# Layer 1's probabilities times v as three products of halves, and PSUM banks of layer 0 emptied ahead of the weight halves

## The reference, cut to what matters

```python
for layer in range(DEPTH):
    mod = cond @ ada_w[layer] + ada_b[layer]
    shift, scale, gate = jnp.split(mod, 3, axis=-1)
    h = rms_norm(x, norm_w[layer]) * (1.0 + scale[:, None, :]) + shift[:, None, :]
    y = moba_branch(...) if layer % N_MIXERS == 0 else mlstm_branch(...)
    x = x + gate[:, None, :] * y
# mlstm, one head: a causal decay matrix times q k^T, and that times v
s_qk = jnp.einsum('bhtd,bhsd->bhts', qc, kc) * jnp.exp(log_D - m_t[..., None])
num = (w_inter[..., None] * jnp.einsum('bhtd,bhde->bhte', qc, C)
       + jnp.einsum('bhts,bhse->bhte', s_qk, vc))
```

## Time and profile before

| | us |
|---|---|
| median of 3 runs | 1528.75 |
| lowest, highest | 1528.12, 1531.22 |
| the profiled execution, whole | 1528.15 |
| its span, first to last instruction | 1526.4 |
| PE busy (DVE, ACT) | 1454.9 (1093.3, 749.9) |
| mean granted PE clock | 0.989 |

### The profile page before, as it was taken

One profiled execution on the slowest core, in us unless ns is written; L12 is line 12 of the kernel. 1 busy time (PEld: TensorE's weight loads), 2 busy tenths in 40 slices (PEclk: granted clock), 3 DMA queues, 4 the chain that ended last, 5 costly groups with the idle time before them and its releaser, 6 DMA issues.

```text
span 1526.4 us, 18995 instructions
## 1 busy us (share of the span) xinstructions
PE 1454.9 (95%) x6655; PEld 1196.5 (78%) x6655; DVE 1093.3 (72%) x1208; ACT 749.9 (49%) x1024; POOL 45.4 (3%) x78
## 2 busy tenths in 40 slices
PE   2788999999999997999999999999999999999998
PEld 2577788878888876778888888888888888888886
DVE  5898698998989796687866566556556556556557
ACT  3554456544545546555454454454454454554552
POOL 1000010101000000010000000000000000000000
PEclk9899999999999999999999999999999999999999
DMA  9999779987999954698856566556556556556653
GB/s 313 376 355 340 271 269 329 331 310 279 319 326 322 317 167 127 225 351 293 272 179 193 166 190 194 167 186 192 172 182 193 175 179 193 177 179 193 179 179 111
DMA packets 199230, 361.47 MB, mean 237 GB/s; under 512 B 14224, under 2 KB 48360, under 8 KB 199164
## 3 DMA queue, kind: packets, MB, share of 16 engines
q1 hardware_dynamic: 198112, 359.60, 71.8%
q10 hardware_dynamic: 1056, 1.06, 0.2%
HBM read 358.51 MB, written 2.11 MB: 236 GB/s over the span
## 4 chain that ended last, share of the span: by engine, by line
PE 77%; issue 10%; DVE 5%; ACT 4%; DMA 3%; POOL 0%; SPq 0%; ACTq 0%; DVEq 0%; POOLq 0%
PE proj L1286 22%; PE proj L1288 22%; PE proj L1287 22%; DVE ada_acc L824 2%; PE mix L1286 2%; PE mix L1288 2%; PE mix L1287 2%; DMA raw<-in_att_w_in 1%; DMA ada_raw<-in_ada_w 1%; ACT w_hi L535 1%; PE mix L1405 1%; DVE w_lo L805 1%; PE mix L1520 1%; PE mix L1472 1%; ACT work L623 1%
## 5 line engine op out<-in xcount | busy, mean ns | idle before, releaser
L805 DVE TENSOR_TENSOR w_lo<-raw,w_hi 128x1024 fp32r<-128x1024 f32 x480 | 586.7, 1224 | 388.1 <-ACT w_hi L535 387.6
L535 ACT ACTIVATE w_hi<-raw 128x1024 fp32r<-128x1024 f32 x480 | 507.8, 1061 | 694.6 <-PE proj L1288 571.6
L1286 PE MATMUL proj<-w_hi,h_hi 128*128 128x512 f32 x1472 | 587.8, 399 | 8.6 <-DVE h_lo L870 5.4
L1288 PE MATMUL proj<-w_hi,h_lo 128*128 128x512 f32 x1472 | 575.9, 391 | 0.0
L1287 PE MATMUL proj<-w_lo,h_hi 128*128 128x512 f32 x1472 | 575.6, 391 | 0.0
L1286 PEld LDWEIGHTS proj<-w_hi,h_hi 128*128 128x128 f32 x1472 | 277.7, 189 | 70.3 <-issue 7.4
L1287 PEld LDWEIGHTS proj<-w_lo,h_hi 128*128 128x128 f32 x1472 | 277.9, 189 | 59.0 <-issue 3.3
L1288 PEld LDWEIGHTS proj<-w_hi,h_lo 128*128 128x128 f32 x1472 | 277.8, 189 | 58.8
L824 DVE SCALAR_TENSOR_TENSOR ada_acc<-ada_raw,cond,ada_acc 128x1024 f32<-128x1024 f32 x180 | 230.3, 1280 | 10.2 <-DMA ada_raw<-in_ada_w 8.7
L1286 PE MATMUL proj<-w_hi,y_hi 128*128 128x512 f32 x320 | 126.1, 394 | 2.4 <-DVE stream L968 2.4
L1288 PE MATMUL proj<-w_hi,y_lo 128*128 128x512 f32 x320 | 124.6, 390 | 0.0
(11 more groups left out here) (198 smaller groups left out, 879.7 us busy)
## 6 DMA issues: line engine op xcount, KB each, us to landing
ada_raw<-in_ada_w SPq DMA_DIRECT2D x192, 512.0 KB, 6.2
raw<-in_mlstm_w_in SPq DMA_DIRECT2D x192, 512.0 KB, 3.7
raw<-in_att_w_in SPq DMA_DIRECT2D x128, 512.0 KB, 7.2
raw<-in_mlstm_w_in SPq DMA_DIRECT2D x128, 256.0 KB, 3.0
raw<-in_mlstm_w_out SPq DMA_DIRECT2D x64, 512.0 KB, 4.3
raw<-in_att_w_out SPq DMA_DIRECT2D x32, 512.0 KB, 6.1
stream<-in_x SPq DMA_DIRECT2D x4, 512.0 KB, 9.6
ada_raw<-in_x SPq DMA_DIRECT2D x4, 512.0 KB, 7.5
```

What stands on the lines that cost most here:

```text
L535: act.activation(w_hi[:, c % LEAD, :], raw[:, c % LEAD, :], ACT.Copy).then_inc(hi_ready, 1)
L805: dve.tensor_tensor(w_lo[:, c % LEAD, :], raw[:, c % LEAD, :], w_hi[:, c % LEAD, :].bitcast(F32), ALU.subtract).then_inc(lo_ready, 1)
L1286: pe.matmul(out_, a_hi, b_hi, start=start, stop=False, **kw)
L1288: return pe.matmul(out_, a_lo, b_hi, start=False, stop=stop, **kw)
```

## The change

Two things change.

In layer 1, `pv1` no longer multiplies in true fp32. ACT's copies out of PSUM now round to fp32r (`v1_hi`, `pT1_hi`); DVE subtracts these from what stands in PSUM (`v1_rest` at step 15 behind `p1_out`, `pT1_rest` at step 18), and PE does three products for each of the three. The wait of `pv1` is now for DVE's halves. Space for `v1_lo` is that of the rope tables of layer 0.

In layer 0, `run` gets a second table, `first`, whose tasks of step i come ahead of `prepare`. The four `z_copy` of ACT, and the nine `z_add` and twelve `out_evac0` of DVE, go from the old table into it.

```diff
@@ buffers
-        rope_a = sb("rope_a", [P, 2, NT, HD])
-        rope_b = sb("rope_b", [P, 2, NT, HD])
+        with ExitStack() as layer0_only:
+            rope_a, rope_b = (layer0_only.enter_context(nc.sbuf_tensor(n, [P, 2, NT, HD], F32))
+                              for n in ("rope_a", "rope_b"))
+        v1_lo = sb("v1_lo", [P, NT, NC], F32R)
...
+        v1_hi = sb("v1_hi", [P, NT, NC], F32R)
...
+        pT1_hi = sb("pT1_hi", [P, 3 * P], F32R)
...
+        pT1_lo = sb("pT1_lo", [P, 3 * P], F32R)
@@ ACT, layer 1
         def pT1_evac(act, h):
             act.wait_ge(pt1_done, h + 1)
-            act.activation(pT1, mix[1][:, 0:3 * P], ACT.Copy).then_inc(pT1_ready, 1)
+            act.activation(pT1_hi[:], mix[1][:, 0:3 * P], ACT.Copy).then_inc(pT1_hi_ready, 1)
+
+        def v1_evac(act, h, end):
+            act.wait_ge(granule_used, end)
+            act.activation(v1_hi[:], both[1][:], ACT.Copy).then_inc(v1_hi_ready, 1)
...
-                    15: [lambda: copy_evac(act, 1, end(1), v1)],
+                    15: [lambda: v1_evac(act, h, end(1))],
@@ the steps
-        def run(eng, prepare, it, base, n, tasks, start=0):
+        def run(eng, prepare, it, base, n, tasks, start=0, first={}):
             for i in range(start, n):
+                for task in first.get(i, []):
+                    task()
                 prepare(eng, it, base + i + LEAD)
                 for task in tasks.get(i, []):
                     task()
@@ ACT, layer 0
-                {i: [lambda j=j, i=i: z_copy(act, j, i)] for j, i in Z_COPIES},
...
-            run(act, hi, 0, 0, NG0, layer0, -LEAD)
+            run(act, hi, 0, 0, NG0, layer0, -LEAD, {i: [lambda j=j, i=i: z_copy(act, j, i)] for j, i in Z_COPIES})
@@ DVE, layer 1
+        def v1_rest(dve, h):
+            dve.wait_ge(v1_hi_ready, h + 1)
+            dve.tensor_tensor(v1_lo[:], both[1][:], v1_hi[:].bitcast(F32), ALU.subtract).then_inc(in_evac, 1)
+
+        def pT1_rest(dve, h):
+            dve.wait_ge(pT1_hi_ready, h + 1)
+            dve.tensor_tensor(pT1_lo[:], mix[1][:, 0:3 * P], pT1_hi[:].bitcast(F32), ALU.subtract).then_inc(pT1_ready, 1)
...
-                          {15: [lambda: p1_out(dve, h)], 25: [lambda: y1_part(dve, h)], y_at: [lambda: y1_out(dve, h)]})
+                          {15: [lambda: p1_out(dve, h), lambda: v1_rest(dve, h)],
+                           18: [lambda: pT1_rest(dve, h)], 25: [lambda: y1_part(dve, h)], y_at: [lambda: y1_out(dve, h)]})
@@ DVE, layer 0
-                {i: [lambda args=args: z_add(dve, *args)] for args in Z_ADDS for i in args[1:2]},
...
-                {first + 2 * q + 1: [lambda o=o, q=q, first=first: out_evac0(dve, o, q, first + 2 * q + 1)]
-                 for o, first in enumerate(outs) for q in range(CHUNKS)},
...
-            run(dve, lo, 0, 0, NG0 - LEAD, layer0, -LEAD)
+            sums = merged(
+                {args[1]: [lambda args=args: z_add(dve, *args)] for args in Z_ADDS},
+                {first + 2 * q + 1: [lambda o=o, q=q, first=first: out_evac0(dve, o, q, first + 2 * q + 1)]
+                 for o, first in enumerate(outs) for q in range(CHUNKS)})
+            run(dve, lo, 0, 0, NG0 - LEAD, layer0, -LEAD, sums)
@@ PE, layer 1
-            pe.matmul(mix[2][:], pT1[:, 0:P], v1[:, 0, :], start=True, stop=True)
-            pe.matmul(mix[3][:], pT1[:, P:2 * P], v1[:, 0, :], start=True, stop=False)
-            pe.matmul(mix[3][:], pT1[:, 2 * P:3 * P], v1[:, 1, :], start=False, stop=True).then_inc(pv1_done, 1)
+            for i, (bank, t, start, stop) in enumerate(((2, 0, True, True), (3, 0, True, False), (3, 1, False, True))):
+                w = slice(i * P, (i + 1) * P)
+                op = three(pe, mix[bank][:], pT1_hi[:, w], pT1_lo[:, w], v1_hi[:, t, :], v1_lo[:, t, :], start, stop)
+            op.then_inc(pv1_done, 1)
```

More of the change, by code:

```diff
@@ L176, in build @@
         stat = sb("stat", [P, 112])
-        work = sb("work", [P, 9728 + 4 * (SEQ + 3)])
+        with ExitStack() as shared_space:
+            work = shared_space.enter_context(nc.sbuf_tensor("work", [P, 9728 + 4 * (SEQ + 3)], F32))
+        sb("work_cv", [P, 1024])
+        v1_hi = sb("v1_hi", [P, NT, NC], F32R)
+        sb("work_gates", [P, 5888 - 2048])
+        pT1_hi = sb("pT1_hi", [P, 3 * P], F32R)
+        sb("work_decays", [P, 9344 - 6272])
+        pT1_lo = sb("pT1_lo", [P, 3 * P], F32R)
+        sb("work_rest", [P, 4 * (SEQ + 3)])
         def part(a, n, pat=None, **kw):
@@ L210, in build @@
         cv = part(0, 1024, "p (j t) -> p j t", j=4)
-        v1 = part(1024, 1024, "p (t n) -> p t n", t=NT)
         o1 = part(2048, 1024, "p (t n) -> p t n", t=NT)
@@ L216, in build @@
         p1 = part(5504, 384)
-        pT1 = part(5888, 384)
         a_bc = part(6272, H1 * 384, "p (h n) -> p h n", h=H1)
@@ L315, in build @@
         qk_turned, qk_padded = (sem(n) for n in ("qk_turned", "qk_padded"))
+        v1_hi_ready, pT1_hi_ready = (sem(n) for n in ("v1_hi_ready", "pT1_hi_ready"))
         c_in, conv_turned, norm_turned = (sem(n) for n in ("c_in", "conv_turned", "norm_turned"))
```

## The result

The changed kernel takes 1514.81 us, the median of 4 runs (1514.44 to 1515.22). The kernel before, timed on the same chip, takes 1529.82 us. The ratio is 0.990, with a 95% interval of 0.989 to 0.992. The forecast was 1516.5 in a range of 1510 to 1524. The profiled execution's span fell from 1526.4 to 1512.7 us, by 13.7 where the forecast had 12.2. The medians differ by 15.0 us, since before's profiled execution was 1.7 us quicker than this median of it.

What follows compares the result with a forecast made beforehand. The tensor engine, busy 95%, was taken as the bound. Layer 0 gains 6.0 (order) + 3.5 (clock) + 1.1 (c78) = 10.6 us, products 4.1, head 0 loses 2.5: 12.2 us, from 1528.75 to 1516.5, range 1510 to 1524.

Steps and rivals of the forecast that it cites:

- c5: Layer 0, granule c5: earlier ACT copy shortens PE's 5.00 us stop; 0.9 us kept of 0 to 5.75, loads being the limit.
- c19: Layer 0, granule c19: DVE's sum starts earlier, 1.5 us gained; stop stays near 2 us and its slow spell remains.
- Rival 3: Better than forecast: no head 0 wait (1514.0), or the spells at c19 and c22 go too (1513.0); chance 0.17.
- c22 and c29: Layer 0: column sums behind c21 come 0.4 us earlier; granule c29's sum starts 1.4 us earlier.
- c34 and c36: Layer 0: stops of 0.9 us each, at granule c34 and the column sums behind c36, vanish; 1.8 us together.
- rival 1: Clock stays low where it was and head 0's new stop brings a spell: 7 us gained, 1521.8; chance 0.17.
- c78: Layer 0, granule c78: PE's 2.4 us stop shrinks by 1.1 us; the other eleven L968 sums end no stop.
- Rival 4: Slower: pushed hi and lo halves come late, 28.2 us if PE feels each, 1544.8; chance 0.05.
- The products: Layer 1, pv1: nine products at 0.23 us replace 2.58 us of fp32 matmuls; 0.51 x 8 heads = 4.1 us gained.
- Rival 5: Layer 1: the nine products run at 0.43 us steps, 3.87 us against 2.58; 1530.9; chance 0.03.
- Head 0: Layer 1, first head: pv1 waits for pT_lo behind DVE's backlog; 2.5 us lost, bounds 0 and 4.2.
- the clock term: Layer 0: the slow spells behind the stops of c29 and c36 go; 2 x 1.75 = 3.5 us, bounds 0 and 7.

Runs made afterwards that it cites:

- experiments 1 and 7: 1 is l0_only; 7, against the changed kernel, left six of nine matmuls a head out of pv1, keeping only the hi-half product: ratio 0.9836.
- pT_first: From the changed kernel, head 0's pT_lo made on DVE ahead of the w_lo of the same step: ratio 0.9916.
- zadds_only: From the kernel before, only DVE's nine layer 0 sums L840 (z_add) moved ahead of the lo halves: ratio 0.9932.
- outsums_only: Experiment 5: from the kernel before, only DVE's twelve sums into the stream (L968, out_evac0) moved ahead of the lo halves: ratio 0.9999.
- after_again: The changed kernel run once more, unaltered: ratio 0.9899 to the kernel before, span 1513.0 us.
- experiment 2: The run l1_only: from the kernel before, only the layer 1 part, nine products of halves, with layer 0 as before: ratio 0.9991.
- l1_only: The same run as experiment 2: from the kernel before, only the layer 1 products of halves: ratio 0.9991.
- h10_first: From the changed kernel, ACT's step 10 making of h and DVE's following h_rest moved ahead of their steps' weight halves: ratio 0.9932.
- l0_only: From the kernel before, only the layer 0 part, copies and sums ahead of the halves, pv1 in true fp32: ratio 0.9923.
- copies_only: From the kernel before, only ACT's four layer 0 copies moved ahead of the hi halves: ratio 0.9986.
- zadds_again: zadds_only run once more, unaltered, against the kernel before: ratio 0.9932.

## Why the prediction was right, point by point

**The bound.** PE's stops and the clock in layer 0, PE's own work in the loop. Both held: experiments 1 and 7.

**c5: 0.9 forecast.** The stop of 5.0 and its spell went whole (from c4 to c5 5.2 us), then a stop at c8 (0.8), a wait of the column sums behind c10 for `ada_acc` (1.7), a new spell at c11 (with the stop at c12 2.6) and the steps behind it (0.4) took back all but 1.1 us by c14 (-0.14 against +0.98 at c0). The five other executions with this layer 0 keep 1.5 to 2.8. The small value was near, and its reason holds in part: ACT waits 1.6 to 4.2 us for loads before most of these hi halves, but 1.6 us of what went back was a spell, which the reason didn't have. That spell stands at c11 in all eight profiles in which the copies go first, and in none of the other five. Taken alone the copies give more, 1.6 by c14 and 2.3 by c19.

**c19: 1.5 forecast, without its spell.** From c14 to c19 2.05, and the spell 1.6 more (c19 to c20). The forecast kept the spell, since the stop stays near 2 us; pT_first (2.13) and zadds_only (2.38) have it, the changed kernel in both executions has not. With the changed layer 0 it is missing in five executions of six, so the 1.6 us are likely, and not sure. Rival 3 counted on this and on c22's; c22 kept its own.

**c22 and c29: 0.4 and 1.4.** From c20 to c29 together 1.4 us. The column sums' stop fell by 0.1 only (2.17 to 2.09), so 0.4 was 0.3 too much, and c29's stop by 1.3 (2.40 to 1.13): its term was right.

**c34 and c36: 1.8, and two spells of 1.75.** c29's spell gave 1.4 (c29 to c30); c30 to c38, with c34's stop, c36's and the spell at c37, 4.2, against 1.8 + 1.75 = 3.55. zadds_only shows the same two numbers, 1.4 and 4.2: they come from the nine sums. But outsums_only, where the z sums stand as before, had no spell at c29 either (stop 2.15), so a part of the 1.4 can fall to chance. That the clock stays up at a short stop, and that rival 1 was wrong, is in the windows: 1.00.

**c78: 1.1.** Measured 1.15, and 1.17 in outsums_only. That the other eleven end no stop is not contradicted. The 1.05 us ahead of c66 come from DVE's backlog ahead of L940 (experiment 5), which comes and goes between executions. In all c38 to c78 gave 2.7 us (2.0 in after_again), 1.6 more than this term.

**No half comes late.** Right: c51 kept its 0.17 us, and PE's waits for w_lo are three of 2.0 us in all, where before had three of 2.2. Rival 4 is out. None of PE's waits in layer 0 ends on one of the 25 pushed halves in the view of waits.

**The products: 0.51 x 8.** Measured 0.45 x 8 = 3.6, by the heads' periods, in a run with layer 0 undisturbed (experiment 2) and in the change. The rows have 2.58 and 2.09, 0.49. A product costs 0.23 to 0.24 us here. The Trainium skill, page "TensorE: Matmul & The Clock Gate", section "Back-to-back issue gap", gives N / 2.4 + 2.5 ns for an isolated matmul at the full clock, 216 ns for 512 columns, and about 131 ns in a sustained stream; the trace agrees with neither, since 512 columns take 227 to 230 ns here. With 216 ns the gain would have been 8 x (2.58 - 1.94), an estimated 5.1 us. Rival 5 is out by the same rows.

**Head 0: a new wait of 2.5, range 0 to 4.2.** The chain of DVE was worked out correctly: pT_lo was to end at 659.6, and 646.95 + 12.64, the shift of head 0, is 659.59. The size at PE was off, because PE came later than assumed: scores' spell and stop together took 1.7 + 0.7 = 2.4 us. Where the scores have no spell (l1_only, h10_first) the wait is 2.31 and 2.35 us, with a spell behind it, and head 0 loses 3.1 and 2.9. Where they have one, PE comes late and waits 0.7. But the scores' spell isn't the products' work: l0_only, without them, has it too and loses 1.6 us in head 0, and copies_only and outsums_only lose 2.9 each, while zadds_again, with a stop of 2.88 us and no spell, loses nothing. So of the changed kernel's 2.1 us about 0.5 net belongs to the products with their wait. The forecast had 2.5 - 0.5 = 2.0. This was agreement by two errors that cancel, a spell that wasn't foreseen and a wait that it hid, and that is luck.

**The sum.** 13.7 against 12.2. Layer 0 gave 13.7 against 10.6: the step that was mis-sized is the clock term, 3.5 forecast where c19's spell was worth 1.6 more, and the stretch from c38 to c66 with 1.5 that no term had. The 13.7 is also the largest of six executions with this layer 0; the others have 11.7 to 13.4. The products gave 0.5 less than forecast. What no term had on the other side is the norm between the layers: c159 to head 0's silu gives back 1.1 us, with a short new spell in it, and 0.6 in after_again, without one.

Left open: why the kernel's first granule starts 1.0 us later (c0, +0.1 to +1.6 in the runs here, with no relation to the edits that I can name), and why a stop of one length brings a spell in one execution and none in another.

None of the variants with the reference's output beats the change: pT_first, the nearest, overlaps it in interval (0.990 to 0.993 against 0.989 to 0.992) and is not faster.

## What to carry to other kernels

When an engine both prepares the next operands and empties the banks that the tensor engine waits for, put the emptying first wherever the operands have slack; find the slack as the distance between the end of the half and the start of its matmuls, and count only stops that don't end on a load. Three products of halves replace one fp32 matmul at 0.23 us a product against 0.86, where the engine is fully busy and somebody else can make the lo half; look for the place where that somebody has a backlog, since with the products alone one head lost 3.1 us and the seven behind it gave 2.6. And treat an idle gap of 2 to 3 us as a risk of some 1.7 us more, not as a certainty.

## What the runs showed of the hardware

**A stop of one length does and doesn't lower the clock.** With a spell of 0.43 us steps behind it: c19's stop at 2.13 (pT_first), 2.36 and 2.38 (zadds twice), and 3.49 to 3.90 in five profiles; c29's at 2.40 and 2.45; c78's at 2.44. Without: c19's at 2.11 to 2.13 in five profiles, c29's at 2.15, c78's at 2.44 or 2.45 in before, l1_only, copies_only and zadds_again. At the scores: with, at 2.82 to 3.16 in eight profiles; without, at 1.28, 2.73, 2.88, 2.95 and 3.00. Most spells cost 1.65 to 1.7 us, by what their steps have over 0.23; the shortest cost 1.2, and some at c5, c11 and c22 2.2 to 2.6. It can start at once, as at c5, or some matmuls later, as from 303.51 on in zadds_only. One spell more or less is as much as the spread between two executions of a kernel here, so a single profile misleads by that much. No run here changes the chance of a spell by itself, so its cause stays open.

**Emptying PSUM late can cost the clock too.** Four of the five spells of before's layer 0 behind its first granule (c5, c19, c29, c37) stand behind a stop for such a copy (c5, by ACT) or sum (the others, by DVE), and those of c19, c29 and c37 are gone, with the stops cut, in both profiles of the changed kernel; in place of c5's there is one at c11, behind column sums that waited 1.31 us for `ada_acc`. The Trainium skill, page "TensorE: Matmul & The Clock Gate", section "Loop structure matters more than you think", has it that a VectorE copy out of PSUM leaves PE warm; that holds in these traces where PE doesn't have to stand for it, as in the loop (clock 1.00). Where PE stands for a VectorE sum it holds at some stops (before: c34, 0.93 us, and c78, 2.44 us) and not at others (before: c19, 3.85 us, and c29, 2.40 us).

**DVE's prices.** v_lo, 128x1024 out of PSUM, 1.20 us; pT_lo, 128x384, 0.55 us, against 0.46 by size alone.
